# The last projection of a hybrid block by Strassen's scheme, with the weight sums built by accumulating DMA stores in HBM

## What is computed

```python
def reference(x, mem, norm_g, w_in, ..., w_kv_mem, w_br_a, w_br_b, w_br_c, w_out, final_g):
    u = rmsnorm(x, norm_g);  proj = u @ w_in                     # 2048 -> some 14000 columns
    p_a = (gated_deltanet(qkv_a, ...) * silu(z_a)) @ w_br_a      # 1024 -> 2048
    p_b = (s5_layer(x_b, ...)         * silu(z_b)) @ w_br_b
    p_c = (memory_cross_attention(q_c, rmsnorm(mem), w_kv) * silu(z_c)) @ w_br_c
    merged = gates[0] * p_a + gates[1] * p_b + gates[2] * p_c    # [512, 2048]
    h = x + merged @ w_out                                       # 2048 x 2048 weights
    return rmsnorm(h, final_g)
```

## Time and profile before

| | |
|---|---|
| median of three runs | 2096.84 us (2096.5 to 2099.84) |
| profiled execution | 2097.53 us, span 2095.8 us |
| TensorE matmul busy | 2067.8 us, 99% |
| VectorE / ScalarE / GpSimd busy | 60% / 38% / 36% |
| output product, first to last matmul | 1913.76 to 2088.06 us |
| behind the last matmul | 7.7 us |
| DMA | 260.63 MB, mean 124 GB/s |

### The profile page before, as it was taken

The page is one execution under the profiler, slowest core; times in us unless marked ns, Lnnn a source line. Parts: engine busy times, 40 slices in busy tenths (PEclk is TensorE's granted clock), DMA queues, the critical chain, the costliest instruction groups (busy, mean ns, idle before and its releaser), DMA issues.

```text
span 2095.8 us, 30735 instructions
## 1 busy us (share of the span) xinstructions
PE 2067.8 (99%) x12124; PEld 1691.8 (81%) x12124; DVE 1267.3 (60%) x1779; ACT 804.7 (38%) x1055; POOL 744.7 (36%) x555
## 2 busy tenths in 40 slices
PE   7999999999999999999999999999999999999998
PEld 6799888888787787877878778777778888888886
DVE  6554353439688596885968959676433335454333
ACT  5433232353344533445334443453242222232223
POOL 0000000038576585765857658577201000100000
PEclk9999999999999999999999999999999999999999
DMA  8244343453343433434334343343356565553334
GB/s 258 61 127 135 102 134 91 114 135 91 104 116 94 121 97 104 115 95 120 97 104 114 96 117 100 104 117 102 103 169 207 173 184 150 180 151 110 112 123 149
DMA packets 382913, 260.63 MB, mean 124 GB/s; under 512 B 23769, under 2 KB 351810, under 8 KB 382146
## 3 DMA queue, kind: packets, MB, share of 16 engines
q1 hardware_dynamic: 364146, 203.16, 35.6%
q0 software_dynamic: 11408, 43.00, 5.9%
q10 hardware_dynamic: 7232, 12.72, 1.6%
HBM read 223.17 MB, written 27.28 MB: 119 GB/s over the span
## 4 chain that ended last, share of the span: by engine, by line
PE 94%; DVE 2%; DMA 1%; ACT 1%; issue 1%; POOLq 0%; ACTq 0%; DVEq 0%
PE bank L456 29%; PE bank L458 28%; PE bank L457 28%; PE bank L1097 1%; PE bank L979 1%; PE bank L991 1%; DMA yst<-s_out 1%; DVE wl L450 1%; PE bank L1046 0%; PE bank L1087 0%; PE bank L952 0%; PE bank L1035 0%; PE bank L1088 0%; PE bank L1077 0%; PE bank L1060 0%
## 5 line engine op out<-in xcount | busy, mean ns | idle before, releaser
L456 PE MATMUL bank<-uh,wh 128*128 128x512 f32 x2048 | 826.1, 403 | 2.9 <-DVE wl L450 2.7
L458 PE MATMUL bank<-uh,wl 128*128 128x512 f32 x2048 | 799.3, 390 | 0.0
L457 PE MATMUL bank<-ul,wh 128*128 128x512 f32 x2048 | 799.0, 390 | 0.0
L450 DVE TENSOR_TENSOR wl<-raw,wh 128x1024 fp32r<-128x1024 f32 x352 | 468.6, 1334 | 476.3 <-ACT wh L442 475.0
L442 ACT ACTIVATE wh<-raw 128x1024 fp32r<-128x1024 f32 x352 | 370.2, 1058 | 552.2 <-DMA raw<-in_w_in_dram 182.0
L456 PEld LDWEIGHTS bank<-uh,wh 128*128 128x128 f32 x2048 | 384.7, 188 | 90.5 <-issue 10.0
L458 PEld LDWEIGHTS bank<-uh,wl 128*128 128x128 f32 x2048 | 384.4, 188 | 83.5
L457 PEld LDWEIGHTS bank<-ul,wh 128*128 128x128 f32 x2048 | 385.2, 188 | 74.1 <-issue 1.9
L622 POOL DMA_DIRECT2D gated_c<-ox x8 | 4.3, 543 | 372.6 <-DVE ox L1808 371.9
L663 POOL TENSOR_TENSOR hr<-tcos,gr 128x512 f32<-128x512 f32 x32 | 51.7, 1615 | 199.4 <-DVE gi L2138 199.3
L1449 ACT ACTIVATE gk<-bank 128x512 f32<-128x512 f32 x48 | 28.7, 598 | 192.0 <-PE bank L458 192.0
(11 more groups left out here) (355 smaller groups left out, 2826.1 us busy)
## 6 DMA issues: line engine op xcount, KB each, us to landing
raw<-in_w_in_dram SPq DMA_DIRECT2D x224, 512.0 KB, 3.9
raw<-in_w_kv_mem_dram SPq DMA_DIRECT2D x32, 512.0 KB, 4.0
raw<-in_w_out_dram SPq DMA_DIRECT2D x32, 512.0 KB, 3.6
gates<-gk ACTq DMA_DIRECT2D x48, 256.0 KB, 4.3
gates<-gates POOLq DMA_DIRECT2D x24, 512.0 KB, 4.7
raw<-in_s_w_glu_dram SPq DMA_DIRECT2D x16, 512.0 KB, 4.0
raw<-in_w_br_c_dram SPq DMA_DIRECT2D x16, 512.0 KB, 3.9
raw<-in_w_br_a_dram SPq DMA_DIRECT2D x16, 512.0 KB, 4.0
```

The source lines that it names most:

```text
L450: dve.tensor_tensor(k.wl[slot][:, c], k.raw[slot][:, c], k.wh[slot][:, c].bitcast(F32), ALU.subtract).then_inc(k.w_lo, 1)
L456: pe.matmul(o, ah, bh, start=start, stop=False)
L457: pe.matmul(o, ah, bl, start=False, stop=False)
L458: return pe.matmul(o, al, bh, start=False, stop=stop)
```

## The change

The output product is done by Strassen's scheme on halves of tokens, inner dimension and output columns. With token halves of 256, inner halves of 1024 and columns taken as pairs of 256 (`QC`) from the left and right half of `w_out`, there are 4 groups `g` of 8 units (one inner tile `t` each). A unit has seven products instead of eight, each of two 128-token pieces, three passes, 256 columns. In the last group two of the seven products (2 and 3) are left out; the token tiles 0 and 1 of the left-out part are done directly at the end (`last_row`), so that less is left to combine. It is 3*8*42 + 8*30 + 96 = 1344 matmuls of 256 columns.

- **Weight sums.** Four of the seven weight operands are sums of quarters of `w_out`. They are built in an HBM tensor `weight_forms` (16.8 MB) by GpSimd DMAs from HBM to HBM: 16 plain copies of 1 MB (`top_left`), then 8 adding DMAs of 1.5 MB (`add_top_right`) in the attention stage, each released by a `w_used` count (about one per weight block, blocks 3 to 10, 12 to 19 and 20 to 27); then per head of the head loop one adding DMA of 1.5 MB (`add_bottom_left`) and one of 0.5 MB (`add_bottom_right`). In these DMAs a piece that is needed in two or three forms is read two or three times.
- **Activation sums.** GpSimd makes three combinations of `merged` tiles (`merged_sums`, 8 times four 128x256 operations); the branch columns are walked in another order so that both tiles of a pair are early. The low-half tiles of branch 2's operand move from `gh` to `uh`.
- **Weights for a unit** come in three DMAs (128 KB, 256 KB, 512 KB), with four slots; in the last group in two, and at the very end four times two pieces of 256 KB (`last_weights`).
- **Combination.** VectorE, ScalarE and GpSimd add the seven PSUM banks of a group into the rows of `hrow`, into which `x` is loaded before. The norm and the stores at the end run in the order of tiles 2, 3, 0, 1.

```diff
+    def top_left(block, t, f):
+        pool.wait_ge(k.w_used, 2 * block)
+        top = k.w_out[t * P:(t + 1) * P, 0:W].unsqueeze(1).to_broadcast([P, 2, W])
+        pool.dma_start(k.forms_d[t, :, f:f + 2, :], top).then_inc(k.w_forms, 16)
+    def add_top_right(block, t):
+        pool.wait_ge(k.w_used, 2 * block)
+        pool.wait_ge(k.w_forms, 16 * 2 * KW)
+        top = k.w_out[t * P:(t + 1) * P, W:D].unsqueeze(1).to_broadcast([P, 3, W])
+        pool.dma_start(k.forms_d[t, :, 0:3, :], top, accum_op=ALU.add).then_inc(k.w_forms, 16)
...
-    with pool.Fori(0, XH - 1) as i:
-        attention_store((i, 0))
+    for b in range(4):
+        top_left(3 + 2 * b, b, 0)
+        top_left(4 + 2 * b, b, 2)
+    attention_store((0, 0))
+    for b in range(4, KW):
+        top_left(4 + 2 * b, b, 0)
+        top_left(5 + 2 * b, b, 2)
+    attention_store((1, 0))
+    for b in range(KW):
+        add_top_right(20 + b, b)
+    attention_store((2, 0))
...
     mixer((HEADS, -1), (HEADS, -2))
+    add_bottom_right(KW - 2)
+    add_bottom_left(KW - 1)
     mixer(None, (HEADS, -1))
+    add_bottom_right(KW - 1)
...
+    def last_weights(v):
+        sp.wait_ge(k.w_used, y_part(UNITS - 4 + v))
+        for i in range(2):
+            sp.dma_start(k.wyr[v][:, 2 * i:2 * i + 2, :], quarters(k, (KW + 2 * v + i) * P, GROUPS - 1)).then_inc(k.w_in_half[v], 16)
...
+        for i in range(2):
+            a, o = slice(i * P, (i + 1) * P), bank[:, i * QC:(i + 1) * QC]
+            mm = pe.matmul(o, hi[:, a], wh, start=t == 0 and i == 0, stop=False)
...
+            pe.matmul(o, hi[:, a], wl, start=False, stop=False)
+            mm = pe.matmul(o, lo[:, a], wh, start=False, stop=t == KW - 1 and i == 1)
...
+    def last_row(i, t):
+        v, bank, a = t // 2, ps[6 + i], slice(i * P, (i + 1) * P)
+        if t % 2 == 0:
+            pe.wait_ge(k.w_lo, last_part(v))
...
+        o = quarter(k, rows, half, g)
+        pool.tensor_tensor(o, o, halves(v[:, 0:S]), ALU.add if part < 2 else ALU.subtract).then_inc(k.o_add, 1)
```

More of the change, by code:

```diff
@@ L1647, in scalar_program @@
                 branch_hi(2, (b,))
[L1648 to L1671 removed]
+            if n == 2 and b in (2, 4, 6):
+                early_hi(b - 2)
+                early_hi(b - 1)
@@ new lines, in scalar_program @@
+            if n == 2 and b in (3, 5):
+                sums_hi(b - 3)
+                sums_hi(b - 2)
+    weights_x(0)
+    sums_hi(4)
+    weights_y(0)
+    sums_hi(5)
+    late, early, sums = LATE, EARLY, SUMS
+    for n in range(UNITS):
+        g, t = divmod(n, KW)
+        if n < len(late):
+            late_hi(late[n][0])
+        if n + 1 < UNITS:
+            weights_x(n + 1)
+        if n == UNITS - 1:
+            last_hi(0)
+        if n < len(late) and len(late[n]) > 1:
+            late_hi(late[n][1])
+        if n + 1 < UNITS:
+            weights_y(n + 1)
+        if t == KW - 1:
+            first_product(g)
+        if n in early:
+            early_hi(early[n])
+        if n in sums:
+            sums_hi(sums[n])
+        if t in (1, 2) and g:
+            for m in (2, 3) if t == 1 else (0, 1):
+                row_squares(g - 1, m)
@@ L1675, in vector_program @@
+LATE = ((0, 1), (2, 3), (4,), (5,), (6, 7))
+EARLY = {2: 6, 3: 7}
+SUMS = {5: 6, 6: 7}
+OPERANDS = [("high", 0), ("high", 1), ("sums", 0), ("sums", 1), ("high", 2), ("high", 3), ("sums", 2), ("sums", 3),
+            ("high", 4), ("high", 5), ("sums", 4), ("sums", 5)]
+for n in range(KW):
+    OPERANDS += [("low", t) for t in (LATE[n] if n < len(LATE) else ())]
+    OPERANDS += [("high", EARLY[n])] if n in EARLY else []
+    OPERANDS += [("sums", SUMS[n])] if n in SUMS else []
 def vector_program(k, dve):
@@ new lines, in vector_program @@
+            if n == 2 and b in (2, 4, 6):
+                early_lo(b - 2)
+                early_lo(b - 1)
+            if n == 2 and b in (3, 5):
+                sums_lo(b - 3)
+                sums_lo(b - 2)
+            if n == 2 and b == KW - 1:
+                weights_x(0)
+                sums_lo(4)
+                weights_y(0)
+                sums_lo(5)
+            merge(n, b)
+    late, early, sums = LATE, EARLY, SUMS
+    for n in range(UNITS):
+        g, t = divmod(n, KW)
+        last = n == UNITS - 1
+        if n < len(late):
+            late_lo(late[n][0])
+        if not last:
+            weights_x(n + 1)
+        if n < len(late) and len(late[n]) > 1:
+            late_lo(late[n][1])
+        if not last:
+            weights_y(n + 1)
+        if n in early:
+            early_lo(early[n])
+        if n in sums:
+            sums_lo(sums[n])
+        if t == KW - 1 and not last:
+            second(g)
+            third(g)
+            sixth(g)
+            seventh(g, 7 * g + 3)
+            fourth(g)
+            fifth_rows(g)
+            fifth_shared(g)
```

493 lines of the change are left out of this document (359 added, 134 removed).

## The result

The changed kernel takes 2155.5 us (median of four, 2151.5 to 2162.2) against 2097.0 for the kernel before: a ratio of 1.028 [1.025, 1.031], slower by 58.6 us. The forecast was 2098 with a range from 2088 to 2134; the result lies outside it. The profiled execution took 2162.2 us.

What follows compares the result with a forecast made beforehand. TensorE's queue was taken as the bound, busy 99% of the span: 2097.5 - 15.9 + 6.3 + 1.0 + 0.5 = 2089.4, plus 8.5 for the HBM work gives 2097.9, say 2098 us, range 2088 to 2134.

Steps and rivals of the forecast that it cites:

- Bound by TensorE, and a wait costs its full length: Whole kernel: TensorE's queue is the time, busy 99% of the span; making it wait costs the full length anywhere.
- Fewer matmuls: Output product: 1344 short matmuls at 0.1177 us, 158.2 us in place of 174.1, a gain of 15.9 us (15 to 17).
- Last weights and tail: End of the output product: 2.6 us of TensorE idleness and a longer tail, together costing 6.3 us (3 to 8).
- Copies, 1 us: Attention's key and value blocks, heads 1 and 2: copies lack 0.2 to 1.0 us each, 0 to 3 us, taken as 1.
- the lead: How long weights are ready before TensorE uses them: 1.8 us at 256 columns, 9.6 us at 512.
- Adding DMAs in the attention, 6 + 1.5 us: Head 3's key and value blocks: 3.7 to 4.9 us each, 6 us lost, plus 1.5 where the first go out together.
- the high end: HBM work at twice the price, 6 us a copy and 9 an adding DMA: up to 50 us in sum.
- The packets: The DMA queues: packets average 558 B on SyncE's queue and 3.8 KB on the software queue.
- Head loop, 0 us: Head loop: 2 MB of adding DMAs per head cost 0, to 5 us per head only at the high price.
- Phase end, 1.0 (0 to 2.5): Before the `yst` load: one more 0.5 MB adding DMA can delay the landing of the `gated_a` store, 1.0 us.
- Starved weights: Key and value blocks, heads 1 to 3: HBM work costs twice, weight halves stand behind it; 2105 to 2140 us, chance 0.31.
- Its own sign: Between 110 and 300 us: TensorE's waits for weights above 15 us, with halves landing after 10 us and more.

Runs made afterwards that it cites:

- place alone: The changed kernel with its copies only in the attention's query and gate blocks, all adds in the head loop, each request waiting for the one before: 2092.1 us.
- paced chain: The changed kernel with each form built in place by 0.5 MB steps, each head-loop step waiting for the one before, no adds in the attention: 2092.3 us.

## Why the prediction failed, step by step

**Bound by TensorE, and a wait costs its full length: right, and too low.** The 50.3 us of waits made the attention 59.5 us longer. The step from waits to time left out the clock: behind three of the waits TensorE worked at a granted clock of 0.50, which explains some 7 of the 9.2 us.

**Fewer matmuls: right, some 2 us short.** The first matmul of the output product starts at 1986.41, the first direct row 1248 matmuls later at 2135.44: 0.1194 us each against the 0.1177 predicted. The sentence beside the sum, "A seventh less would have been 24.9; 9.1 us go to the shorter stream", is wrong, and nothing hangs on it: 1344 short matmuls against 2 * 768 are an eighth less, which would be 21.8 us, and 5.9 go to the shorter stream. (Timeline of TensorE, the last matmul of the products, the first direct one, and the last of all:)

```profile
2135.32 0.28 PE L1473 MATMUL bank<-wh,sxl 128*128 128x256 f32 x1
2135.44 0.28 PE L1499 MATMUL bank<-wh,sxh 128*128 128x256 f32 x1
...
2150.84 0.28 PE L1503 MATMUL bank<-wh,ul 128*128 128x256 f32 x1
```

**Last weights and tail: right in the sum, with one step wrong.** Predicted were 2.6 us of idleness and an end at T + 25.3, T being the end of unit 31. Measured: 2.1 us, and with T = 2135.4 an end at T + 24.9. The timeline shows the chain: `wl` from ScalarE's late `wh`, the fifth product's two additions, GpSimd's subtractions, the square:

```profile
2140.94 1.23 DVE L2588 TENSOR_TENSOR wl<-raw,wh 128x1024 fp32r<-128x1024 f32 x1 [1.92 <-ACT wh L1905]
2142.08 0.68 DVE L2627 TENSOR_TENSOR hrow<-hrow,bank 128x512 f32<-128x512 f32 x1
2142.68 0.68 DVE L2631 TENSOR_TENSOR gk<-gk,bank 128x512 f32<-128x512 f32 x1
...
2142.84 1.29 POOL L946 TENSOR_TENSOR hrow<-hrow,cst 128x512 f32<-128x512 f32 x1 [2.45 <-DVE hrow L2627]
...
2144.09 1.29 POOL L946 TENSOR_TENSOR hrow<-hrow,gk 128x512 f32<-128x512 f32 x1
...
2144.16 0.63 ACT L1920 ACTIVATE cst<-hrow 128x512 f32<-128x512 f32 x1 [1.74 <-POOL hrow L946]
```

But the first square stood behind the first of the two subtractions only, of 1.29 us and not 1.6, and began at T + 8.8; the prediction had it behind both, at T + 10.8. The last scaling began at T + 18.5 (19.6 foretold), and from there to the end it took 6.4 us and not 5.7. So part of the agreement is luck: an early start and slower steps behind it. The direct rows took longer, too, 15.7 us and not 13.9, since the clock is 0.50 at 2144 to 2146 us, behind their wait; the end did not hang on them.

Together the parts outside the HBM work were summed to a gain of 9.1 us (without the 1.0 for the phase end, which the kernel without HBM work doesn't have), and 10.3 were measured.

**Copies, 1 us: wrong, 12.5.** Their price was right: 3.2 us of all engines, in the predicted 2.5 to 3.3. What failed is the step behind it, "the copies then lack 0.2 to 1.0 us each, less the lead". It takes for granted that weights are served first and that a copy has what they leave over. No trace shows them first. Where the adding DMAs stood, both queues moved equal numbers of packets (714 to 715). At 113 to 125 us of the kernel with copies only the numbers are not equal, 2513 packets of loads and 447 of copies, but from 121 to 122 it is 38 of loads to 80 of copies, and a half lands in 8.4 us instead of 4.0, where the lead is 1.8; so TensorE waits although the engines were busy for 0.81 of these 12 us only. The waits in that trace are 5.9 us, and the attention is 8.5 us longer.

**Adding DMAs in the attention, 6 + 1.5 us: wrong, 48.3.** Two mistakes multiply. The first is the price: one takes 9.7 us of all engines, not 3.7 to 4.9; the number that I had for the high end, 9, was the true one. I chose near the low end because `x`, `gst` and `yst` were the measured neighbours. None of them writes to HBM or adds to what stands there; they bounded a copy well (3.2 us in 2.5 to 3.3) and an adding DMA not at all (9.7 us against 3.7 to 4.9). The second is again the share. The run with all adds as copies parts the two: with the first mistake taken away the waits in the attention are 27.2 us and not 50.3. At the true price eight of them need 78 us of engines in the 71 us that I had reckoned with, beside 30 us of loads: they can't fit, and the loads, with half of the packets but a ninth of the bytes (257 to 275 us), were the ones that waited.

**The packets: sizes read right, and no part of the sum.** The queues' packets differ as the earlier trace rows had it, 558 B and 3.8 KB, and the windows of the result show them served in equal numbers, 714 to 715. So they are in two of the experiments: 868 of loads to 855 from 250 to 266 us with all adds as copies, 255 to 256 from 266 to 274 us with 4 KB rows. The traces show equal numbers over some microseconds, not how many make a turn. The nearest row before, a half issued beside `yst` that took up to 11.8 us, three times its 3.9, was no measure of it: it was issued beside 2 MB that needed 12.2 us, so it could not be late by more than that. In the kernel before, from 1535 to 1536 us, the queues moved 59 and 60 packets. A delay near the ratio of the packets' sizes came only where the long packets last longer than the short ones need: beside two adding DMAs in a row (29.0 us to landing, 244 to 256 us) a half took 32.6 us where it takes 4.0 alone. Landing is no price of the engines either: a copy took 3.0 us per MB of them here, though one of 1.5 MB landed after 9.9 us.

**Head loop, 0 us: wrong, 8.4 with the phase end.** Here the price was the high one, and the cost per head still only some 1.1 us (8.6 over eight heads), far from the "to 5 per head": single waits of up to 1.6 us for weights and one of 3.1 us for `dl`. The 8.4 are the difference of two medians; the traces have 8.6 and 2.1. The kernel with place alone puts all 24 adds there and waits 5.9 us for weights.

**Phase end, 1.0 (0 to 2.5): too small, 4.0**, and not by the mechanism named, a delay of the store's landing (the drain begins 4.1 us behind the store's issue, 4.0 before). The drain itself is longer, 6.9 us where it was 3.0, in kernels too that have no request just ahead of it.

**The rivals.** *Starved weights* had the right mechanism and place, the key and value blocks, and it decided from the price that it named (6.5 us for an adding DMA; 9.7 it was). Its own sign came, too: waits above 15 us, with halves landing after more than 10. Its time, 2120, and the range's end of 2134 were too low: even the high end of the HBM work, "up to 50 us", whose terms as written add up to 34 (4 for the copies, 30 for the adding DMAs), credited every block with its lead, as if weights went first, and had nothing for the clock and the head loop. It came to 69.2.

## What to carry to other kernels

Before putting a large DMA beside a stream of loads, compare the packets of the two queues. Here the stream kept its share of packets and not of bytes: 512 B rows beside 4 KB rows made 714 of 1429 packets and got a ninth of the bytes (0.36 of 3.16 MB, 257 to 275 us), and a half took 32.6 us; as 4 KB rows they made 255 of 511 packets, got 0.96 of 1.99 MB (266 to 274 us), and a half took 9.5. Free engine time was no cover: with the engines busy for 0.81 of the time (copies only, 113 to 125 us) a half took 8.4 us in place of 4.0. What told the cases apart was how long the long requests lasted against the lead of the loads that they met. The same 46.1 MB cost 69.2 us where many of the requests met blocks with 1.8 us of lead, two or three of them at once, and 5.7 us one by one where the lead is 9.6 us or the loads are few.

## What the runs showed of the hardware

- Two queues with work moved equal numbers of packets: 715 and 714 in 18 us of the changed kernel (257 to 275 us), with 3.9 KB and 0.5 KB in a packet; 256 and 255 in 8 us of the kernel with 4 KB rows (266 to 274 us), with 4.1 and 3.8 KB. Not so behind the issue of a half at 244.52 us: it moved no packet for 3.5 us.
- An adding DMA from HBM to HBM took 6.2 us of all 16 engines per MB (place alone), a copy 3.0 (copies only). Set apart, with loads beside it, an add of 1.5 MB landed in 14.3 and 15.1 us and a copy of 1.5 MB in 9.9 and 10.0 us.
- During 23.3 us of idleness, up to 325.55 us of the changed kernel, TensorE's granted clock fell to 0.50 (the window 310 to 320), and it stayed there for some 6 us of work (0.50 from 326 to 331, 1.00 from 332); the matmuls of 256 columns stepped by 0.212 us (326.14, then 326.35) instead of 0.118.
- GpSimd's drain at the phase end took from 2.5 us (place alone) to 7.1 us (paced chain) in kernels that differ in their DMAs from HBM to HBM, and 3.0 without any. Why is open.
